# Six gathered rows in each ring instead of four, and the group loops written out, in a transformer encoder layer with expert retrieval

## The chip, the cores and the metric

The program runs on one core of a Trainium2 chip. Its time is the device time of one execution in microseconds (us); below it is the median of three executions. Beside them stands one profiled execution, from which all rows come.

## The reference, cut to what matters

The layer takes 1024 tokens of width 1024 in float32. It normalises them, projects them, runs 8-head latent attention and a 2-D Fourier transform side by side, mixes the two by sigmoid gates, projects, and normalises again (h1). Then comes the retrieval, from which nearly all memory traffic stems:

```python
q = (xt @ w_q).reshape(T, 8, 2, 128)
s_half = jnp.einsum('thcd,hcnd->thcn', q, keys)      # 128 keys per half
sv, si = lax.top_k(s_half, 16)
cand = (sv[:, :, 0, :, None] + sv[:, :, 1, None, :]).reshape(T, 8, 256)
cv, ci = lax.top_k(cand, 16)
expert = (ia * 128 + ib).reshape(T, 8 * 16)          # 128 experts of 16384 per token
gate = jax.nn.softmax(cv, axis=-1).reshape(T, 128)
u = jnp.take(w_u, ec, axis=0)                        # rows of 1024 floats
h = jnp.einsum('cd,ced->ce', xc, u)
a = jax.nn.gelu(h, approximate=False) * gc
y = jnp.einsum('ce,ced->cd', a, jnp.take(w_v, ec, axis=0))
out = layer_norm(alpha * h1 + y)
```

Each of the 1024 tokens needs 128 rows of `w_u` and 128 rows of `w_v`, of 4 KB each: 1.07 GB in all.

## The kernel before, in words

**Tiling.** 128 tokens are a tile, two tiles a group (`TILES`), and there are four groups (`GROUPS`). A prologue computes what all groups need (normalised input, latents, keys K and values V, the Fourier stage). Everything before the retrieval of a group is its *front*; the retrieval sums are its *peer* part. The peer part of group g runs beside the front of group g+1.

**Steps.** A group has 256 steps (`STEPS`), one for each of 2 x 128 slots; a slot is one expert for each of the 128 tokens of a tile. In each step m every engine does, in an order written out in its own program, first its piece of the peer part and then its piece of the front. Engines meet only in semaphores, and each runs its list strictly in order.

The peer piece of a step:
- GpSimd (POOL) issues a gather of 128 rows of `w_u` (`gather_u`, L301) for slot m + 76 and one of `w_v` (`gather_v`, L311) for slot m + 64 (`LEAD` 64, `AHEAD` 12). A gather is an indirect DMA of 512 KB, one 4 KB row to each partition.
- VectorE (DVE) multiplies the u row with h1 and sums it to one number per token (`dot`, L865), and frees the row (`u_free`).
- ScalarE (ACT) applies gelu to 8 slots at a time (L1083), and scales the v row by the coefficient into `av` (`scale`, L1092), which frees the v row (`scaled`).
- TensorE (PE) adds `av` to the accumulator by eight 128x128 transposing matmuls (L592).

**The rings.** Gathered rows lie in two rings, `u_rows` of `NU` = 4 and `v_rows` of `NV` = 4 rows, which share the tensor `rows`. A gather into a ring waits until the row four slots back has been used. On POOL the u gather and the v gather of a step follow one another in one queue, so that a u gather that waits for its row holds up the v gather behind it.

**The front by steps.** Steps 0 to 63 hold attention: a unit of one head and one tile every 4 steps, with scores (PE L475), row maximum (DVE L752), exponential (ACT L1023), transposes (PE L333), a copy (DVE L760) and the product with V (PE L491). For the first tile's eight units a query projection goes before (PE L459, taken out by ACT L1018 and DVE L744). Steps 72 to 119 hold gates and mixing (PE L515, L527, DVE L775), steps 120 to 135 the output projection (L538), from 136 the second normalisation, from 148 the retrieval's query and key scores (PE L559, L567) and the top-16 searches on DVE (`retrieve`, L726 to L854). The second tile's search of a group runs in the steps of the next group.
Weights come in a stream of 52 chunks per group on the SP queue through a ring of four (L244 waits, the next line loads). At step 0 of each group ACT loads the group's queries and rotary table (`load_queries`, L946 and L947), for which PE's first query projection waits.

**Loops.** POOL, PE, DVE and ACT run groups 0 to 2 of the peer part in a hardware loop (`Fori`), with semaphore counts computed in registers, and the last group written out; SP loops over all four groups. The steps before the first group's peer part (`peer(-1, ...)`, front of group 0) are written out as well. Before each gather there is a `nop` which carries the wait.

Of the kernel before, what the change touches and what calls it, by code (L numbers as in the profile page):

```python
# [25 lines left out]
FG, FD = 4, 128  # L26
PH, NK, HALF, TOPK = 8, 128, 128, 16
P = 128
# [11 lines left out]
LEAD = 64  # L40
PAIRS = PH // 2
PSLOTS = SLOTS // PAIRS
NU = NV = 4
NAV = 2
NW = 4
NDFT = 4
# [21 lines left out]
def layer_program(nc, x, lnp, w_lat, w_z, w_kr, b_lat, b_zT, b_krT, gqkv, w_uk, w_uv, b_gate, wstream,  # L68
# [4 lines left out]
    with ctx:  # L73
        def sb(name, shape, dt=fp32):
            return ctx.enter_context(nc.sbuf_tensor(name, shape, dt))
# [34 lines left out]
        bg = sb("bg", [P, 2, KD])  # L110
        rowsum = sb("rowsum", [P, TILES, H])
        rrow = sb("rrow", [P, TILES, H])
        nmax = sb("nmax", [P, 2])
        sv = sb("sv", [P, TILES, 2 * PH, TOPK])
        si = sb("si", [P, TILES, 2 * PH, TOPK], u32)
        cv = sb("cv", [P, TILES, PH, TOPK])
# [1 line left out]
        cab = sb("cab", [P, 2, PSLOTS])  # L118
        cabi = sb("cabi", [P, 2, PSLOTS], u32)
        iota16 = sb("iota16", [P, TOPK])  # L120
        altern = sb("altern", [P, 1])
        ymid = sb("ymid", [P, FG])
        gsum = sb("gsum", [P, 2])
        ids_peer = sb("ids_peer", [P, TILES, SLOTS], i32)
        gate_front = sb("gate_front", [P, TILES, SLOTS])
        gate_peer = sb("gate_peer", [P, TILES, SLOTS])
# [1 line left out]
        act_out = sb("act_out", [P, 2, BATCH])  # L128
        coef = sb("coef", [P, 2, BATCH])
        st = sb("st", [P, 3, 12])  # L130
        mv = sb("mv", [P, 3, 2])
        sd = sb("sd", [P, 3, 2])
        rq = sb("rq", [P, 4])
        gqk = sb("gqk", [P, 2, 2])
        bz = sb("bz", [P, FG])
        bkr = sb("bkr", [P, 1])

        s2_flat = S2[:, :, :, :].rearrange("p t c n -> p t (c n)")
        probs, probsT = s2_flat[:, 0, 0:S], s2_flat[:, 0, S:2 * S]
# [2 lines left out]
        onehot = sb("onehot", [P, PSLOTS, TOPK])  # L142


        hT_all = rows
        zcs = rows[:, :, :].rearrange("p t (g c) -> p t g c", g=FG)
        zT = hh
        w_lat_sb = S2[:, :, :, :].rearrange("p t c n -> p (t c n)").rearrange("p (k n) -> p k n", k=KD)
        w_z_sb = wring[:, :, :].rearrange("p a b -> p (a b)").rearrange("p (k n) -> p k n", k=KD)
# [74 lines left out]
        def positive(v):  # L224

            return not isinstance(v, int) or v > 0

        def slot_of(g, i):

            return (g + 1, i - STEPS) if i >= STEPS else (g, i)  # L230
# [10 lines left out]
        @block.sync  # L241
        def _(sp):
            def load(dst, src, s):
                sp.dma_start(dst, src).then_inc(s, 16)  # L244

            load(ident[:, :], ident_in, consts_in)
            load(x_t[:, 0, :], x[tok(0), :], x_in[0])
            for j in range(3):
                load(ln0[:, j, :], lnp[j:j + 1, :].to_broadcast([P, D]), ln0_in)
            load(blat, b_lat[0:1, :].to_broadcast([P, 512]), ln0_in)  # L250
            load(w_lat_sb, w_lat, w_lat_in)
            load(x_t[:, 1, :], x[tok(1), :], x_in[1])
            for dst, src in ((gqk[:, :, :], gqkv), (bz[:, :], b_zT), (bkr[64:128, :], b_krT),
                             (bg[:, :, :], b_gate), (iota16[:, :], iota_in), (dftc, dft_ch), (altern[:, :], altern_in)):
                load(dst, src, consts_in)
            load(w_z_sb, w_z, w_z_in)
            load(w_kr_sb, w_kr, w_z_in)
            load(w_uk_sb, w_uk, w_kv_in)
            load(w_uv_sb, w_uv, w_kv_in)
            load(rope_all[64:128, :], rope_tab, rope_in)  # L260
            for i in range(2, TT):
                sp.wait_ge(h0_done, i - 1)
                load(x_t[:, i % 2, :], x[tok(i), :], x_in[i % 2])
            sp.wait_ge(h0_done, TT)
            load(keys_sb, peer_keys.rearrange("c n d -> n c d"), keys_in)


            def stream(g):
                for c in range(CHUNKS):
                    sp.wait_ge(w_free, g * CHUNKS + c + 1)  # L270
                    n = 512 if c < WM0 else D
                    load(wring[:, c % NW, 0:n], wstream[c, :, 0:n], w_in_s[c % NW])

            sp.wait_ge(z_ps, 2 * FG)
            with sp.Fori(0, GROUPS) as g:
                stream(g)


# [1 line left out]
        def _(pool):  # L280
# [13 lines left out]
            def gather_u(g, i):  # L294
                g, i = slot_of(g, i)
                if i % PSLOTS == 0:
                    pool.wait_ge(handed, g * TILES * PAIRS + i // PSLOTS + 1)
                pool.wait_ge(u_free, g * STEPS + i + 1)
                pool.nop(nofuse=True)
                t, s = divmod(i, SLOTS)  # L300
                pool.indirect_dma_start(  # L301
                    u_rows[:, i % NU, :], None, peer_u,
                    bass.IndirectOffsetOnAxis(ap=ids_peer[:, t, s:s + 1], axis=0)).then_inc(u_in[i % NU], 16)

            def gather_v(g, i):
                g, i = slot_of(g, i)

                pool.wait_ge(scaled, g * STEPS + i + 1)
                pool.nop(nofuse=True)
                t, s = divmod(i, SLOTS)  # L310
                pool.indirect_dma_start(  # L311
                    v_rows[:, i % NV, :], None, peer_v,
                    bass.IndirectOffsetOnAxis(ap=ids_peer[:, t, s:s + 1], axis=0)).then_inc(v_in[i % NV], 16)

            def peer(g, last):
                for m in range(STEPS):
# [3 lines left out]
                        gather_v(g, m + LEAD)  # L320

            peer(-1, False)
            with pool.Fori(0, GROUPS - 1) as g:
                peer(g, False)
            peer(GROUPS - 1, True)

# [2 lines left out]
        def _(pe):  # L329
# [273 lines left out]
            for m in range(STEPS):  # L603
# [1 line left out]
                    peer(-1, m + LEAD)  # L605
                front(0, m)
                dft(m)
            with pe.Fori(0, GROUPS - 1) as g:
                for m in range(STEPS):
                    for t in range(TILES):  # L610
                        if m + LEAD == (t + 1) * SLOTS:
                            turn_back(g, t)
                    peer(g, m + LEAD)
                    front(g + 1, m)
# [8 lines left out]
        def _(dve):  # L623
# [169 lines left out]
            def retrieve(g, t, m, t0, period):  # L793

                for h in range(PH):
                    a = t0 + period * h
                    for c in range(2):
                        if m == a + c:
                            if c == 0:
                                dve.wait_ge(s_sb, g * 2 * PH + 2 * h + 2)  # L800
                                dve.nop(nofuse=True)
                            topk(S2[:, t, 2 * h + c, :], sv[:, t, 2 * h + c, :], si[:, t, 2 * h + c, :])
                    if m == a + 2:
                        dve.drain()
# [54 lines left out]
            def dot(g, i):  # L859
                g, i = slot_of(g, i)  # L860
                t = i // SLOTS
                dve.wait_ge(u_in[i % NU], g * (16 * STEPS // NU) + 16 * (i // NU + 1))
                row = u_rows[:, i % NU, :]
                b = i // BATCH % 2
                v.tensor_tensor_reduce(out=row, in0=row, in1=h1_peer[:, t, :], scale=1.0, scalar=0.0, op0=ALU.mult,  # L865
                                       op1=ALU.add, accum_out=dots[:, b, i % BATCH:i % BATCH + 1]).then_inc(u_free, 1)
# [61 lines left out]
                    if not last:  # L928
                        front(g + 1, m)

            with dve.Fori(0, GROUPS - 1) as g:
                group(g, False)
            group(GROUPS - 1, True)

# [2 lines left out]
        def _(act):  # L937
# [147 lines left out]
            def scale(g, i):  # L1085
                g, i = slot_of(g, i)
                if i % BATCH == 0:
                    act.wait_ge(coef_done, g * (STEPS // BATCH) + i // BATCH + 1)
                act.wait_ge(v_in[i % NV], g * (16 * STEPS // NV) + 16 * (i // NV + 1))
                act.wait_ge(av_free, g * STEPS + i + 1)  # L1090
                b = i // BATCH % 2
                s.activation(av[:, i % NAV, :], v_rows[:, i % NV, :], ACT.Copy,  # L1092
                             scale=coef[:, b, i % BATCH:i % BATCH + 1]).then_inc(scaled, 1)

            def evict(g, t):
# [53 lines left out]
                        if m + LEAD == (t + 1) * SLOTS + 2:  # L1149
                            store(g, t)  # L1150

            with act.Fori(0, GROUPS - 1) as g:
                group(g, False)
            group(GROUPS - 1, True)
            act.wait_ge(stored, 16 * (TT + 1))
# [84 lines left out]
```

## Time and profile before

| what | value |
|---|---|
| median of 3 executions | 3776.41 us (3761.76, 3776.41, 3784.91) |
| the profiled execution's own time | 3791.07 us |
| its span, first to last instruction | 3789.0 us |
| mean granted TensorE clock | 0.808 of full speed |
| busy, share of the span | PE 74%, PE weight loads 58%, DVE 59%, ACT 43%, POOL 62% |
| moved by DMA | 1241.31 MB, 328 GB/s over the span |
| of it by the gathers (queue 0) | 1073.87 MB |

The busy shares are means over stages with different limits. The gathers run from 541.9 us to the end, so that the share of POOL within that stretch is larger than 62%. A row of a wait says which engine and line waited for which; a row of the chain is a piece of the work that ended last.

### The profile page before, as it was taken

To read this page: it belongs to the slowest core of one execution; us is meant where nothing else is said; L and a number is where in the kernel's file an instruction comes from. 1 tells how busy PE (TensorE), PEld (TensorE's weight loads), DVE (VectorE), ACT (ScalarE), POOL (GpSimd) and SP (SyncE) were. 2 spreads that over 40 slices of the span, in tenths; PEclk is the share of its full clock that TensorE was granted. 3 is DMA by queue.
4 is the path that set the end of the run, shared out by engine and by line. 5 is a ranking of instruction groups with operands and counts; after the bars stand their busy time and mean duration, and the time that the engine had idled before them with its cause. 6 is when DMAs were issued, how large, how long until landed. Compare 5 with 4: busy or idle time off the path is not lost.

```text
span 3789.0 us, 45875 instructions
## 1 busy us (share of the span) xinstructions
PE 2797.3 (74%) x14008; PEld 2205.7 (58%) x14008; DVE 2224.2 (59%) x5004; ACT 1619.1 (43%) x1842; POOL 2342.6 (62%) x2075
## 2 busy tenths in 40 slices
PE   6999976677788676577788776677787776665666
PEld 3455855556676565466675665466675665554554
DVE  5143057457765686367666685467765685466643
ACT  1121014445454454355454454455454454444444
POOL 4000017766567778666667777666667777777775
PEclk9999987578799897588799896688898985555556
DMA  4224449989999999989999999899999999999998
GB/s 166 87 100 162 154 149 340 359 317 319 326 404 408 395 382 356 355 313 321 345 400 407 387 388 355 326 325 318 368 398 408 387 376 364 379 362 340 355 390 313
DMA packets 350484, 1241.31 MB, mean 328 GB/s; under 512 B 38481, under 2 KB 46161, under 8 KB 349713
## 3 DMA queue, kind: packets, MB, share of 16 engines
q0 software_dynamic: 294912, 1073.87, 75.6%
q1 hardware_dynamic: 34096, 117.94, 8.5%
q10 hardware_dynamic: 21216, 46.40, 3.4%
q8 instruction: 119, 1.95, 0.2%
q14 instruction: 141, 1.15, 0.1%
HBM read 1222.33 MB, written 15.73 MB: 327 GB/s over the span
## 4 chain that ended last, share of the span: by engine, by line
issue 25%; DMA 25%; PE 20%; POOL 11%; DVE 9%; ACT 5%; DVEq 4%; POOLq 0%; SPq 0%; ACTq 0%
DMA rows<-in_peer_v,ids_peer 15%; DMA rows<-in_peer_u,ids_peer 8%; POOL rows L311 5%; POOL rows L301 5%; ACT av L1092 3%; PE acc L592 3%; DVE rows L865 3%; PE fA L515 2%; PE fA L475 2%; PE m L363 2%; PE fB L527 1%; PE acc L581 1%; PE m L559 1%; DVE nmax L752 1%; PE fB L333 1%
## 5 line engine op out<-in xcount | busy, mean ns | idle before, releaser
L592 PE MATMUL acc<-ident,av 128*128 128x128 f32 x8192 | 1476.5, 340 | 873.9 <-ACT av L1092 860.2
L592 PEld LDWEIGHTS acc<-ident,av 128*128 128x128 f32 x8192 | 1208.8, 176 | 1162.1 <-ACT av L1092 1097.0
L1092 ACT ACTIVATE av<-rows,coef 128x1024 f32<-128x1024 f32 x1024 | 1168.2, 1146 | 1330.4 <-DMA rows<-in_peer_v,ids_peer 1235.1
L865 DVE CUSTOM_DVE_ANT_0 rows<-rows,hh 128x1024 f32<-128x1024 f32 x1024 | 1244.1, 1223 | 786.1 <-DMA rows<-in_peer_u,ids_peer 769.4
L301 POOL DMA_INDIRECT rows<-in_peer_u,ids_peer x1024 | 1110.4, 1084 | 926.5 <-DVE ids_peer L845 348.9
L311 POOL DMA_INDIRECT rows<-in_peer_v,ids_peer x1024 | 1184.2, 1156 | 356.5 <-issue 305.5
L559 PE MATMUL m<-hT_g,wring 128*128 128x256 f32 x1024 | 251.5, 402 | 1.1 <-ACT hT_g L1054 1.1
L515 PE MATMUL fA<-hT_g,wring 128*128 128x256 f32 x1024 | 236.2, 386 | 0.0
L559 PEld LDWEIGHTS m<-hT_g,wring 128*128 128x128 f32 x1024 | 204.5, 205 | 30.4 <-ACT hT_g L1054 1.5
L515 PEld LDWEIGHTS fA<-hT_g,wring 128*128 128x128 f32 x1024 | 195.2, 195 | 25.7
L1023 ACT ACTIVATE S<-fA,nmax 128x1024 f32<-128x1024 f32 x64 | 71.3, 1114 | 191.2 <-DVE nmax L754 191.1
L491 PEld LDWEIGHTS m<-V,S 128*128 128x128 f32 x1024 | 127.3, 201 | 11.4 <-issue 7.2
L760 DVE COPY S<-fB 128x1024 f32<-128x1024 f32 x64 | 78.2, 1221 | 94.5 <-PE fB L333 92.5
L491 PE MATMUL m<-V,S 128*128 128x64 f32 x1024 | 128.3, 281 | 3.4 <-DVE S L760 3.4
L475 PE MATMUL fA<-KT,hT_g 96*128 96x512 f32 x256 | 127.3, 621 | 0.0
L527 PE MATMUL fB<-yo,wring 128*128 128x256 f32 x512 | 121.4, 392 | 0.0
L752 DVE TENSOR_REDUCE nmax<-fA 128x1 f32<-128x1024 f32 x64 | 78.3, 1224 | 67.9 <-PE fA L475 67.9
L527 PEld LDWEIGHTS fB<-yo,wring 128*128 128x128 f32 x512 | 99.6, 198 | 13.7
L1083 ACT ACT_TABLE_LOAD x76 | 97.5, 1283 | 1.3
L775 DVE TENSOR_TENSOR prod<-sg,fB 128x512 f32<-128x512 f32 x32 | 21.9, 685 | 128.2 <-PE fB L527 128.0
L1062 ACT ACTIVATE qcT<-m 128x256 f32<-128x256 f32 x64 | 24.5, 383 | 148.4 <-PE m L559 148.4
L333 PE MATMUL fB<-ident,S 128*128 128x128 f32 x512 | 83.4, 318 | 1.0 <-issue 0.8
(153 smaller groups left out, 2190.8 us busy)
## 6 DMA issues: line engine op xcount, KB each, us to landing
wring<-in_wstream SPq DMA_DIRECT2D x192, 512.0 KB, 6.8
ln<-in_dft_seq ACTq DMA_DIRECT2D x32, 512.0 KB, 3.6
rows<-in_peer_u,ids_peer POOLq DMA_INDIRECT x1024, 6.5
rows<-in_peer_v,ids_peer POOLq DMA_INDIRECT x1024, 6.6
hT_g<-in_x SPq DMA_DIRECT2D x8, 512.0 KB, 4.0
hres_spill<-KT ACTq DMA_DIRECT2D x8, 512.0 KB, 2.7
hT_spill<-rows ACTq DMA_DIRECT2D x1, 4096.0 KB, 11.1
wring<-in_wstream SPq DMA_DIRECT2D x16, 256.0 KB, 6.0
```

The costliest lines, as they stand in the source:

```text
L301: pool.indirect_dma_start(u_rows[:, i % NU, :], None, peer_u, bass.IndirectOffsetOnAxis(ap=ids_peer[:, t, s:s + 1], axis=0)).then_inc(u_in ...
L311: pool.indirect_dma_start(v_rows[:, i % NV, :], None, peer_v, bass.IndirectOffsetOnAxis(ap=ids_peer[:, t, s:s + 1], axis=0)).then_inc(v_in ...
L333: return nc.tensor.transpose(out_, in_, ident[:, :])
L475: last = mm(fA[:, half * 512:(half + 1) * 512], qT_g[0:QK, h, tok(qt)], KT[0:QK, h, half * 512:(half + 1) * 512], start=True, stop=True)
L491: last = mm(m1[:, h * VD:(h + 1) * VD], probsT[:, tok(k)], V[:, k, h * VD:(h + 1) * VD], start=k == 0, stop=k == TT - 1)
L515: last = mm(gb[:, j * GROUP:(j + 1) * GROUP], w[:, tok(k)], hT_g[:, k, :], start=k == 0, stop=k == KD - 1)
L527: last = mm(yb[:, j * GROUP:(j + 1) * GROUP], w[:, tok(4 * j + k)], src[:, k, :], start=k == 0, stop=k == 3)
L559: last = mm(m0[:, (qc % 2) * GROUP:(qc % 2 + 1) * GROUP], w[:, tok(k)], hT_g[:, k, :], start=k == 0, stop=k == KD - 1)
L592: last = mm(acc[:, tok(k)], av[:, i % NAV, tok(k)], ident[:, :], is_transpose=True, start=i % SLOTS == 0 and k % 4 == 0, stop=i % SLOTS == ...
L752: v.reduce_max(nmax[:, u % 2:u % 2 + 1], fA[:, :], AX)
L865: v.tensor_tensor_reduce(out=row, in0=row, in1=h1_peer[:, t, :], scale=1.0, scalar=0.0, op0=ALU.mult, op1=ALU.add, accum_out=dots[:, b, i ...
L1092: s.activation(av[:, i % NAV, :], v_rows[:, i % NV, :], ACT.Copy, scale=coef[:, b, i % BATCH:i % BATCH + 1]).then_inc(scaled, 1)
```

## The change

`NU` and `NV` go from 4 to 6. The tensor `rows` has one pool of `NU + NV` rows and so grows from 8 to 12 rows, 16 KB more per partition. The space comes from two places: the DMA scratch of the program is set to 4096 bytes per partition (its default is 16384), and ten small tensors, each of which was padded on its own, become slices of one. `hT_all` and `zcs`, which used all of `rows`, use its first 8 rows.

256 steps are no multiple of 6, so that the ring's row and its semaphore count depend on the group: `ring` and `landed` work them out from the slot's number over all groups. With loops that would need registers, so the loops are written out as Python loops in all five programs, with constants for all counts. The `nop` ahead of each gather, and one on DVE before a top-16 search, go.

```diff
-NU = NV = 4
+NU = NV = 6
...
+        small = sb("small", [P, 34])
+        nmax = small[:, 0:2]
...
-        hT_all = rows
-        zcs = rows[:, :, :].rearrange("p t (g c) -> p t g c", g=FG)
+        hT_all = rows[:, 0:KD, :]
+        zcs = hT_all.rearrange("p t (g c) -> p t g c", g=FG)
...
+        def ring(g, i, n):
+            return (g * STEPS + i) % n
+        def landed(g, i, n):
+            return 16 * ((g * STEPS + i) // n + 1)
...
-            with sp.Fori(0, GROUPS) as g:
+            for g in range(GROUPS):
                 stream(g)
...
                 pool.wait_ge(u_free, g * STEPS + i + 1)
-                pool.nop(nofuse=True)
                 t, s = divmod(i, SLOTS)
                 pool.indirect_dma_start(
-                    u_rows[:, i % NU, :], None, peer_u,
-                    bass.IndirectOffsetOnAxis(ap=ids_peer[:, t, s:s + 1], axis=0)).then_inc(u_in[i % NU], 16)
+                    u_rows[:, ring(g, i, NU), :], None, peer_u,
+                    bass.IndirectOffsetOnAxis(ap=ids_peer[:, t, s:s + 1], axis=0)).then_inc(u_in[ring(g, i, NU)], 16)
...
                 pool.wait_ge(scaled, g * STEPS + i + 1)
-                pool.nop(nofuse=True)
...
-            with pool.Fori(0, GROUPS - 1) as g:
+            for g in range(GROUPS - 1):
                 peer(g, False)
...
-            with pe.Fori(0, GROUPS - 1) as g:
+            for g in range(GROUPS - 1):
...
                                 dve.wait_ge(s_sb, g * 2 * PH + 2 * h + 2)
-                                dve.nop(nofuse=True)
...
-                dve.wait_ge(u_in[i % NU], g * (16 * STEPS // NU) + 16 * (i // NU + 1))
-                row = u_rows[:, i % NU, :]
+                dve.wait_ge(u_in[ring(g, i, NU)], landed(g, i, NU))
+                row = u_rows[:, ring(g, i, NU), :]
...
-                act.wait_ge(v_in[i % NV], g * (16 * STEPS // NV) + 16 * (i // NV + 1))
+                act.wait_ge(v_in[ring(g, i, NV)], landed(g, i, NV))
                 act.wait_ge(av_free, g * STEPS + i + 1)
...
-    nc = bacc.Bacc("TRN2", target_bir_lowering=False, num_devices=1)
+    nc = bacc.Bacc("TRN2", target_bir_lowering=False, num_devices=1, dynamic_dma_scratch_size=4096)
```

## Rows read from the trace of the kernel before

**Rows 1.** The page: GB/s moved in each of 40 equal slices of the span.
```profile
GB/s 166 87 100 162 154 149 340 359 317 319 326 404 408 395 382 356 355 313 321 345 400 407 387 388 355 326 325 318 368 398 408 387 376 364 379 362 340 355 390 313
```

**Rows 2.** Groups of instructions: count | busy us, mean ns | idle before, its releasers. The gathers.
```profile
L311 POOL DMA_INDIRECT rows<-in_peer_v,ids_peer x1024 | 1184.2, 1156 | 356.5 <-issue 305.5 <-ACT av L1092 38.8 <-DVE dots L865 12.2
L301 POOL DMA_INDIRECT rows<-in_peer_u,ids_peer x1024 | 1110.4, 1084 | 926.5 <-DVE ids_peer L845 348.9 <-DVE dots L865 280.8 <-issue 252.2
```

**Rows 3.** Stretches: length, busy us of PE, PEld, DVE, ACT, POOL, clock, DMA share, GB/s.
```profile
542.00:800.00 258.00, 162.41 (x751) 132.37 (x750) 155.99 (x384) 99.34 (x113) 178.86 (x158) 0.66 0.92 335
800.00:1050.00 250.00, 188.52 (x1104) 157.79 (x1103) 179.82 (x389) 129.51 (x144) 157.69 (x146) 0.84 0.92 327
1050.00:1250.00 200.00, 163.82 (x904) 130.02 (x901) 121.69 (x268) 97.80 (x102) 140.29 (x125) 0.99 1.02 406
1250.00:1600.00 350.00, 239.80 (x1280) 202.57 (x1280) 220.83 (x532) 164.76 (x186) 264.98 (x232) 0.77 0.98 372
1600.00:1850.00 250.00, 184.15 (x1043) 152.49 (x1044) 173.19 (x360) 127.53 (x144) 151.85 (x139) 0.80 0.89 315
1850.00:2050.00 200.00, 168.78 (x926) 139.15 (x925) 121.29 (x289) 99.14 (x104) 144.48 (x125) 0.97 1.01 398
2050.00:2400.00 350.00, 245.59 (x1307) 204.34 (x1306) 229.01 (x545) 167.93 (x189) 267.62 (x236) 0.79 0.99 381
2400.00:2700.00 300.00, 213.32 (x1209) 175.50 (x1210) 198.06 (x421) 148.40 (x165) 183.07 (x170) 0.81 0.89 318
2700.00:2900.00 200.00, 167.04 (x905) 133.70 (x903) 119.62 (x267) 97.23 (x101) 141.92 (x124) 0.97 1.02 401
2900.00:3400.00 500.00, 344.99 (x1727) 286.37 (x1727) 315.14 (x745) 232.70 (x252) 386.79 (x344) 0.70 0.99 376
3400.00:3789.00 389.00, 244.44 (x1108) 196.70 (x1106) 208.57 (x456) 170.32 (x167) 276.93 (x255) 0.60 0.94 351
```

**Rows 4.** Timeline of POOL: start, duration, instruction [idle before]; first in a loop, then written out.
```profile
2398.32 1.01 POOL L301 DMA_INDIRECT rows<-in_peer_u,ids_peer  x1 [0.30 <-issue]
...
3501.48 0.93 POOL L301 DMA_INDIRECT rows<-in_peer_u,ids_peer  x1 [0.30 <-issue]
```

**Rows 5.** Who waited for whom: us in total, times, longest; the two gather waits, 2400 to 2700.
```profile
ACT av L1092 <- DMA rows<-in_peer_v,ids_peer: 70.8, 38, 5.4
POOL rows L301 <- DVE dots L865: 67.9, 27, 8.6
```

**Rows 6.** Timeline of PE in the attention steps of the third loop pass.
```profile
2451.30 1.88 PE L475 MATMUL fA<-KT,hT_g 96*128 96x512 f32 x4
...
2457.01 1.85 PE L592 MATMUL acc<-ident,av 128*128 128x128 f32 x8 [1.21 <-ACT av L1092]
2458.65 1.91 PE L459 MATMUL m<-cqT_g,wring 128*128 128x256 f32 x4
2462.07 1.10 PE L592 MATMUL acc<-ident,av 128*128 128x128 f32 x8 [1.50 <-ACT av L1092]
...
2464.75 1.88 PE L475 MATMUL fA<-KT,hT_g 96*128 96x512 f32 x4
```

**Rows 7.** The chain that ended last, in order of time, shortly after: start, us, what.
```profile
2474.10 9.01 DMA rows<-in_peer_v,ids_peer
...
2492.39 1.73 PE fA L475 x4
```

**Rows 8.** The chain at the loop's turn, around 2412 us.
```profile
2412.41 2.58 issue
...
2421.56 8.03 DMA rope_g<-in_rope_tab
```

**Rows 9.** From issue to landing of the u gathers, all of them.
```profile
DMA to landing us min/median/max: 4.1/6.5/12.0
```

**Rows 10.** The page: the queues that fetch the program's instructions: packets, MB, share.
```profile
q8 instruction: 119, 1.95, 0.2%
q14 instruction: 141, 1.15, 0.1%
```

More of the change, by code:

```diff
@@ L112, in layer_program @@
         rrow = sb("rrow", [P, TILES, H])
-        nmax = sb("nmax", [P, 2])
         sv = sb("sv", [P, TILES, 2 * PH, TOPK])
@@ L120, in layer_program @@
         iota16 = sb("iota16", [P, TOPK])
-        altern = sb("altern", [P, 1])
-        ymid = sb("ymid", [P, FG])
-        gsum = sb("gsum", [P, 2])
         ids_peer = sb("ids_peer", [P, TILES, SLOTS], i32)
@@ L130, in layer_program @@
         st = sb("st", [P, 3, 12])
[L131 to L136, printed above, removed]
+        small = sb("small", [P, 34])
+        nmax = small[:, 0:2]
+        altern = small[:, 2:3]
+        ymid = small[:, 3:7]
+        gsum = small[:, 7:9]
+        mv = small[:, 9:15].rearrange("p (a b) -> p a b", b=2)
+        sd = small[:, 15:21].rearrange("p (a b) -> p a b", b=2)
+        rq = small[:, 21:25]
+        gqk = small[:, 25:29].rearrange("p (a b) -> p a b", b=2)
+        bz = small[:, 29:33]
+        bkr = small[:, 33:34]
         s2_flat = S2[:, :, :, :].rearrange("p t c n -> p t (c n)")
@@ L308, in gather_v @@
                 pool.wait_ge(scaled, g * STEPS + i + 1)
-                pool.nop(nofuse=True)
                 t, s = divmod(i, SLOTS)
                 pool.indirect_dma_start(
-                    v_rows[:, i % NV, :], None, peer_v,
-                    bass.IndirectOffsetOnAxis(ap=ids_peer[:, t, s:s + 1], axis=0)).then_inc(v_in[i % NV], 16)
+                    v_rows[:, ring(g, i, NV), :], None, peer_v,
+                    bass.IndirectOffsetOnAxis(ap=ids_peer[:, t, s:s + 1], axis=0)).then_inc(v_in[ring(g, i, NV)], 16)
             def peer(g, last):
@@ L929, in group @@
                         front(g + 1, m)
-            with dve.Fori(0, GROUPS - 1) as g:
+            for g in range(GROUPS - 1):
                 group(g, False)
@@ L1088, in scale @@
                     act.wait_ge(coef_done, g * (STEPS // BATCH) + i // BATCH + 1)
-                act.wait_ge(v_in[i % NV], g * (16 * STEPS // NV) + 16 * (i // NV + 1))
+                act.wait_ge(v_in[ring(g, i, NV)], landed(g, i, NV))
                 act.wait_ge(av_free, g * STEPS + i + 1)
                 b = i // BATCH % 2
-                s.activation(av[:, i % NAV, :], v_rows[:, i % NV, :], ACT.Copy,
+                s.activation(av[:, i % NAV, :], v_rows[:, ring(g, i, NV), :], ACT.Copy,
                              scale=coef[:, b, i % BATCH:i % BATCH + 1]).then_inc(scaled, 1)
@@ L1150, in group @@
                             store(g, t)
-            with act.Fori(0, GROUPS - 1) as g:
+            for g in range(GROUPS - 1):
                 group(g, False)
```

## The prediction

> **What bounds the kernel now.** I read the slices of the page first. Up to slice 6 the rate is 87 to 166 GB/s, from then on 313 to 408 [rows 1]: the kernel is a prologue of 542 us and then 3247 us of gathering. The change touches the prologue only in where tensors lie, so the question is what sets the pace behind it.
>
> The second view is the two gather groups on POOL [rows 2]. A gather costs POOL 1.084 us (u) or 1.156 us (v), and before each of them there is a gap of 0.30 us in which nothing is waited for [rows 4]. So 2048 gathers take 1110 + 1184 + 2048 x 0.30 = 2909 us of POOL's queue, out of 3247 us. POOL is within 10% of being the bound by itself, which its 62% of the span hides.
>
> The third view splits the 3247 us by stage [rows 3]. For each stretch I take length - POOL busy - 0.30 x its gathers: that is what POOL really stood idle.
> - Attention (800 to 1050, 1600 to 1850, 2400 to 2700): 48.5, 56.5 and 65.9 us idle, 171 us together, at only 315 to 327 GB/s.
> - Gates and projection (1050 to 1250, 1850 to 2050, 2700 to 2900): 22, 18 and 21 us idle, 61 us together, at 398 to 406 GB/s. No slice of the page goes above 408: here the transfers are the bound, and POOL waits because rows come late.
> - The search steps (1250 to 1600, 2050 to 2400, 2900 to 3400): 15, 12 and 10 us idle, 37 us together. POOL is the bound, at 372 to 381 GB/s.
> - The start (542 to 800): 32 us. The end (3400 to 3789): 36 us, of which about 20 lie behind the last gather.
>
> So more rows in flight can help only where POOL waits for a row, and only if neither the transfers nor another chain of work sets the pace there.
>
> **The attention stretches** hold half of the idle time, and look like a shortage of rows: from 2400 to 2700 POOL waited 67.9 us for dots, and ACT 70.8 us for v rows [rows 5]. But whose wait is on the path? A unit is 4 steps. From one score matmul (2451.30) to the next (2464.75) are 13.45 us. In it PE waits 1.21 and 1.50 us for ACT's scaling [rows 6], and what ACT was behind both times is the front itself: scores, maximum on DVE, exponential, then the scaling that is next on ACT's list; and the query projection, which ACT takes out before it scales. No gather is in that circle. The next units do have one, a v gather of 9.01 us [rows 7], and yet the scores of 2451.30 and 2492.39 [rows 6, 7] lie 41.1 us apart for three units, 13.7 us each. The gather wait runs beside a chain that is almost as long. A unit loses about 0.3 us by it on that evidence.
>
> **The change, part by part.**
> - *Rings in attention.* 16 units a group at 0.3 us would be 5 us; the second tile's units also wait for DVE's searches and vary more, so I take 0.5 us each: 8 us a group, 24 us for three groups. The ends are 0 and all of POOL's idle time, 171 us. I stay near the low end, as the unit without a gather is the row that fits the pace.
> - *Leaving attention.* POOL is held up by full rings there, so with six it enters the next stage two slots further on in each ring. Those four gathers (2.1 MB) were moved while there was room, and need not be moved in the stage at the ceiling: 2.1 MB at 408 GB/s is 5.1 us a group, 15 us for three. Bounds 0 and twice that.
> - *Gates and projection.* Transfers bind. From a mean of 402 to 408 GB/s would be 1.5% of 600 us, 9 us; I take 6.
> - *Search steps.* The 37 us are short waits at tile ends and in DVE's searches. A ring two slots deeper absorbs waits shorter than two steps, which are four gathers of POOL at 1.42 us, 5.7 us; transfers have 7% room to 408 GB/s. I take 20, bounds 0 and 37.
> - *Start and end.* Of 32 and 16 us, 11: the first gathers are limited by four rows, but also by the front beside them.
> - *Loops written out.* At the turn of the loop POOL's chain shows 2.58 us of issue [rows 8]. Two turns, an entry and an exit: 8 us, bounds 0 and 15. Inside the pass registers and counts cost nothing visible: the gap before a gather is 0.30 us in the loop and in the written-out group alike [rows 4]. For the same reason I cost the removed `nop` at nothing: the gap stays the same with register arithmetic ahead of it or none. If it did save the 0.03 us of one queue entry, 2048 times, that would be 61 us; that end goes into the range. The code fetch stays as it is: 3.10 MB were fetched for 45,875 instructions [rows 10], 68 bytes each, so passes through a loop are already fetched each time. If fetching did stall, it would be in the written-out last group, where POOL runs without a pause.
> - *A moved load.* The rotary load at step 0 takes 8.03 us on the path [rows 8], among at most 8 gathers in flight. With up to 12 it may take 2 us longer: -6 us for three groups, bounds 0 and -12.
> - *Weight stream on SP.* It too lands later, but three chunks are loaded ahead, at least six steps of about 3 us; the cover is larger than the 12 us of the slowest gather's landing [rows 9]. Nothing.
> - *Packed small tensors, a moved `rows`.* No engine's work changes. Nothing.
> - *Scratch.* Up to 8 gathers are in flight with 16384 bytes, and no row shows POOL waiting for room; with a quarter of it and 12 in flight no row of this trace can say. Nothing, with a rival below.
>
> Gain: 24 + 15 + 6 + 20 + 11 + 8 - 6 = 78 us. The profiled execution took 3791.07 us, 14.7 us above the median of 3776.41. Against its own time the changed kernel comes to 3713, against the median to 3698.
>
> On the scratch, the Trainium skill (DMA: Bandwidth & Descriptors, The descriptor swizzle) says that a 128-partition transfer writes 9 read and 9 write descriptors on each engine, of 16 bytes each; by that my estimate is 256 places, 28 gathers, in the smaller scratch, and it would not bind. No run here shows it yet.
>
> **Rivals.**
> - *The rings are the bound in attention* (20%). For it: 171 us of idle POOL, and the chain through a 9 us v gather. Against it: the 13.45 us unit. If it holds, attention gives back its 171 us instead of 24: 225 us in all, 3551 by the median. The floor of this case: each stretch of [rows 3] takes the longer of its length less POOL's idle time and its bytes at 408 GB/s. From the first stretch to the last that is 226, 202, 199, 335, 194, 195, 338, 234, 197, 490 and 373 us, 2982 in place of 3247, 265 us saved: 3511. With 130 us saved it is 3646.
> - *Nothing moves* (21%). Transfers and POOL bind wherever the front does not, the stored slots are given back in the next stage, and only the loop turns are saved: 3738 to 3790. It would also come so if the transfers were at their ceiling over the whole stretch. The 11 stretches move 1171 MB in 3247 us, 361 GB/s; were that the ceiling, no ring could help: 3776. Against it stand 398 to 406 GB/s for 200 us on end, three times [rows 3]; it has 3 of the 21%. The Trainium skill (SBUF — State Buffer, Summary: rules for kernel authors) says to estimate HBM to SBUF by about 358 GB/s; by that the 1171 MB would need 3271 us and the kernel would already stand at the bound. The trace, with 406 GB/s, disagrees.
> - *The smaller scratch holds POOL up* (9%), the case on the other side. Place: each gather, on POOL. It decides when the scratch has room for fewer gathers than the rings. If room is what 8 in flight just fitted in, a quarter holds 2, and a gather could be issued every 4.1 / 2 = 2.05 us at the shortest landing [rows 9]: 542 + 2048 x 2.05 = 4740 us. With room for 4 at the median landing it is 6.5 / 4 = 1.63 us each, 3870 us by the profiled execution, 3855 by the median. It would show as idle time of POOL with no row free to blame, and longer gathers.
>
> **How the numbers follow.** The forecast's own case (gain 40 to 120 us) has 50% and gives 3656 to 3736; the rings as bound 20%; nothing 21%; slower 9%. A change of 1% (38 us) is about what a measurement of this kernel can tell from none. Faster by more than that is the first two cases, 70%; within 1%, 21%; slower, 9%. The range of 3600 to 3785 leaves out the deep end of the second case, half of its chance, and the slower one. The 61 us of the `nop` would move the forecast to 3637, within it.
>
> **What would show it.** Right: attention stretches still at about 13.2 to 13.6 us a unit, with ACT's wait for v rows mostly gone and POOL still idle there; the search steps without POOL idle time; gates at 405 GB/s or above with the gathers' landing longer than the 6.5 us of before; the 2.6 us of issue at the turns gone. Wrong: units of 12 us or less in attention (the ring was the bound), a gap before gathers other than 0.30 us (the `nop` or the scratch), or gathers longer than 0.94 us without DVE beside them.

## The result, and the profile after

The changed kernel took 3664.82 us (median of 4 runs, 3655.13 to 3692.76) against 3769.09 us before on the same chip (3759.08 to 3784.91): ratio 0.9735, 95% interval 0.970 to 0.977. By the ratio that is 100 us; the two medians lie 104 us apart. The forecast was 3698 us, within 3600 to 3785; the gain was 78 us forecast and 100 us measured. The profiled execution took 3666.81 us, its span is 3665.0 us, 124 us shorter than the profiled span of before. The profiled execution of before was the slowest of its four and 22 us above their median, so what is read from these two traces adds up to more than the 100 us.

First the page, the slices of the changed kernel, as in [rows 1]:

```profile
GB/s 170 92 92 144 172 125 341 384 344 327 330 399 409 409 409 386 376 340 317 360 409 409 409 393 376 374 338 328 373 409 409 409 382 373 408 364 357 359 396 344
```

Ten slices now stand at 408 or 409 GB/s where two of before reached 408, and none goes above. The troughs of 317 to 344 GB/s are still there. They are the attention steps.

The two gather groups, as in [rows 2] (count | busy us, mean ns | idle before):

```profile
L310 POOL DMA_INDIRECT rows<-in_peer_u,ids_peer x1024 | 1151.3, 1124 | 828.2 <-DVE ids_peer L852 348.9 <-issue 276.0 <-DVE dots L872 203.3
L319 POOL DMA_INDIRECT rows<-in_peer_v,ids_peer x1024 | 1156.7, 1130 | 318.9 <-issue 278.1 <-ACT av L1099 40.8
```

POOL's wait for dots fell from 281 to 203 us, and that number still holds the 0.30 us of each gap. To have POOL's time exactly, I took all 2048 gathers of the timeline and split the time from the first to the last into their lengths, gaps of 0.30 us, and what is left:

| kernel | gathers' lengths | gaps | POOL idle | profiled run |
|---|---|---|---|---|
| before | 2296 us | 617 us | 312 us | 3791.07 us |
| after | 2309 us | 617 us | 176 us | 3666.81 us |

The gain is POOL's idle time, 136 us, less 13 us by which the gathers became longer in sum. The gap is the same 617 us without the `nop`, with constants and in a quarter of the scratch:

```profile
2301.93 0.94 POOL L319 DMA_INDIRECT rows<-in_peer_v,ids_peer  x1 [0.30 <-issue]
2303.18 1.01 POOL L310 DMA_INDIRECT rows<-in_peer_u,ids_peer  x1 [0.30 <-issue]
```

Where in the steps did the time come from? PE's rows give marks that are the same steps in both kernels: the first and last scores of a group, the first output projection, the first query projection of the retrieval, and its last one. A mark is the start of such a block of matmuls. The sums are worked out from the timelines.

| stretch (sum over groups) | before | after | gain |
|---|---|---|---|
| first gather to first scores of group 1 | 246.3 | 234.3 | 12 |
| scores, first to last (3 groups) | 614.9 | 595.8 | 19 |
| last scores to output projection (3) | 591.1 | 568.9 | 22 |
| output projection (3) | 255.5 | 253.3 | 2 |
| retrieval queries, first to last (3) | 546.1 | 524.8 | 21 |
| last query to the next group's first scores, over the turn (2) | 310.7 | 290.1 | 21 |
| last query of group 3 to the end | 682.6 | 657.5 | 25 |

With the 2 us by which the first gather came sooner that is the 124 us between the two spans.

Two attention stretches of the changed kernel and one of gates, columns as in [rows 3]:

```profile
1570.00:1767.00 197.00, 154.92 (x920) 130.29 (x918) 140.77 (x287) 108.98 (x125) 132.98 (x120) 0.84 0.93 328
2361.00:2559.00 198.00, 155.58 (x917) 131.47 (x916) 140.72 (x287) 108.67 (x124) 133.85 (x119) 0.83 0.92 327
2559.00:2749.00 190.00, 155.41 (x907) 136.24 (x906) 135.83 (x332) 98.45 (x107) 141.97 (x118) 0.94 1.00 390
```

And the waits in the third group's attention (who waited for whom: us in total, times, longest). The first four lines are the kernel before, from 2437 to 2643, the first to the last scores; the others are the changed kernel, from 2361 to 2559:

```profile
PE acc L592 <- ACT av L1092: 51.4, 35, 3.3
POOL rows L301 <- DVE dots L865: 43.6, 20, 3.6
ACT av L1092 <- DMA rows<-in_peer_v,ids_peer: 41.8, 25, 4.1
ACT S L1023 <- DVE nmax L754: 32.0, 15, 3.7
```

```profile
ACT S L1030 <- DVE small L762: 53.7, 15, 6.5
PEld acc L600 <- ACT av L1099: 46.7, 26, 3.4
PE acc L600 <- ACT av L1099: 39.0, 26, 3.3
POOL rows L310 <- DVE dots L872: 34.5, 21, 3.4
```

The stretch of [rows 5] is 100 us longer, as it holds the turn and the first gates, and its 70.8 us are 41.8 us here. This wait of ACT for v rows has gone from the list altogether. But ACT now waits 22 us more for the row maximum from DVE (53.7 instead of 32.0 us), and POOL still waits for dots. So ACT's waits for rows were removed, and the attention steps became 3% shorter.

The gates can be split further. From the first gate matmul to the output projection 63.2, 63.4 and 63.3 MB were moved in 157.4, 158.8 and 161.3 us before, and 61.9, 62.1 and 61.5 MB in 153.3, 153.9 and 152.9 us after. Each group thus moves 1.5 MB less there, about three gathers, at 403 instead of 398 GB/s. At the ceiling the missing bytes are 11 us for three groups, and the better rate 6 us.

The turn of the loop, as in [rows 8], from the chain that ended last:

```profile
2337.13 1.01 POOL rows L310
2338.14 0.30 issue
2338.45 6.56 DMA rows<-in_peer_v,ids_peer
...
2345.68 8.22 DMA rope_g<-in_rope_tab
...
2353.94 2.09 PE m L467 x4
```

The 2.58 us of issue are gone. The rotary load takes 8.22 us instead of 8.03 and is still on the path; over the three groups it takes 8.40 instead of 8.27 us in the mean.

### The profile page after: what moved, and what is told of

Its sections match the earlier page's. It is cut to its first block, busy times and chain, and to the rows that moved or that the text cites. A ratio compares the mean times of both kernels' runs of the same rounds, so it can differ in the third digit from the quotient of the medians.

```text
span 3665.0 us, 40824 instructions
## 1 busy us (share of the span) xinstructions
PE 2779.8 (76%) x14008; PEld 2205.7 (60%) x14008; DVE 2220.9 (61%) x5004; ACT 1612.2 (44%) x1842; POOL 2356.0 (64%) x2075
## 3 DMA queue, kind: packets, MB, share of 16 engines
q0 software_dynamic: 294912, 1073.87, 76.7%
## 4 chain that ended last, share of the span: by engine, by line
POOL 29%; PE 24%; DMA 18%; issue 11%; DVE 8%; ACT 5%; DVEq 3%; SPq 0%; ACTq 0%; POOLq 0%
DMA rows<-in_peer_v,ids_peer 17%; POOL rows L310 15%; POOL rows L319 15%; PE acc L600 5%; ACT av L1099 4%; PE fA L483 3%; PE m L567 2%; PE fA L523 2%; PE m L371 2%; DVE small L760 2%; PE acc L589 1%; PE fB L341 1%; DVE rows L872 1%; PE m L467 1%; PE m L499 1%
## 5 line engine op out<-in xcount | busy, mean ns | idle before, releaser
L310 POOL DMA_INDIRECT rows<-in_peer_u,ids_peer x1024 | 1151.3, 1124 | 828.2 <-DVE ids_peer L852 348.9
L319 POOL DMA_INDIRECT rows<-in_peer_v,ids_peer x1024 | 1156.7, 1130 | 318.9 <-issue 278.1
L1030 ACT ACTIVATE S<-fA,small 128x1024 f32<-128x1024 f32 x64 | 71.3, 1114 | 266.1 <-DVE small L762 266.1
L768 DVE COPY S<-fB 128x1024 f32<-128x1024 f32 x64 | 78.2, 1222 | 100.2 <-PE fB L341 98.6
L760 DVE TENSOR_REDUCE small<-fA 128x1 f32<-128x1024 f32 x64 | 78.3, 1223 | 53.0 <-PE fA L483 52.9
L783 DVE TENSOR_TENSOR prod<-sg,fB 128x512 f32<-128x512 f32 x32 | 21.8, 682 | 121.5 <-PE fB L535 121.5
```

The source lines that it names most:

```text
L310: pool.indirect_dma_start(u_rows[:, ring(g, i, NU), :], None, peer_u, bass.IndirectOffsetOnAxis(ap=ids_peer[:, t, s:s + 1], axis=0)).then_ ...
L319: pool.indirect_dma_start(v_rows[:, ring(g, i, NV), :], None, peer_v, bass.IndirectOffsetOnAxis(ap=ids_peer[:, t, s:s + 1], axis=0)).then_ ...
L760: v.reduce_max(nmax[:, u % 2:u % 2 + 1], fA[:, :], AX)
```

## The experiments

Each kernel is the changed one with one edit, unless it says otherwise. The runs fell in three sessions, each on another chip. In the first the kernel before took 3944.41 us, in the second 3774.78 us, in the third 3771.07 us; so times are compared within a session, and ratios are to the kernel before of the same session. Why the first chip takes 4.5% longer for the same program is not known. The first session has r4, r5, u6v4 and u4v6, the second b4, r4b, r6 and u6v4b, the third the rest.

**1. Everything but the rings.**

```diff
-NU = NV = 6
+NU = NV = 4
```

> The changed kernel with four rows in each ring (everything else of the change kept: loops written out, no nop, small scratch, packed tensors). Theory (the rings gave nearly all): 0 to 12 us below the kernel before (ratio 0.997 to 1.000), about 95 us above the changed kernel; POOL idle about 300 us between gathers. Rival (written-out loops and the missing nop gave it): 60 us or more below the kernel before, ratio 0.985 or less, gap before gathers below 0.30 us.

> Four rows in each ring, loops written out, again, now beside the whole change. Theory: 8 to 40 us below the kernel before; its distance to the six-row kernel is what the rings give.

Measured: 3893.36 against 3944.41 us, ratio 0.9906 (0.9867 to 0.9944), and in the second session 3754.11 against 3774.78 us, ratio 0.9945 (0.9925 to 0.9965). So what is not the ring is worth 51 us in the first session, between theory and rival, and 21 us (13 to 28 by the interval) in the second, more than the 8 us that I had allowed. Of the three sessions the whole change ran in the second only. There it lies another 80 us below: that is the rings, four fifths of the gain.

**2. The kernel before and the whole change in the same session,** for their traces.

> The kernel before, unchanged, for a trace from the same chip as the three beside it. Theory: POOL idle between gathers is larger than in the four-row kernel with written-out loops only around the loop's turns (3 to 4 us at each of two turns, an entry and an exit). Rival (registers cost time inside the passes): the surplus is spread over all stages of groups 1 to 3.

> The whole change. Theory after the first four runs (the u ring gives nearly all, the v ring nothing): same time as six u rows with four v rows within 10 us, 55 to 75 us below the four-row kernel. Rival (both rings are needed for the full gain): 20 us or more below six-and-four.

Measured: 3773.17 us (one run) and 3673.69 us, ratio 0.9737 (0.970 to 0.9775): the gain stood again. POOL's account for the second session, made as above:

| kernel | lengths | gaps | idle | profiled run |
|---|---|---|---|---|
| before | 2286 us | 617 us | 305 us | 3773.17 us |
| rings of 4 | 2271 us | 617 us | 278 us | 3732.11 us |
| u 6, v 4 | 2324 us | 616 us | 193 us | 3698.95 us |
| u 6, v 6 | 2315 us | 617 us | 174 us | 3671.15 us |

(The profiled run of the kernel with rings of 4 is the fastest of its 11; their median is 3754 us.) The table shows the rings' work and a part that is given back: idle time falls by 104 us from the second line to the fourth, but the gathers' lengths grow by 44 us. How large the part is stays open: from the kernel before to the whole change they grow by 29 us here and by 13 us in the first pair of traces.

The same marks as above, in us gained, split the gain into the rings and the rest (b4 is the kernel before, r4b the one with rings of 4, r6 the whole change):

| stretch | whole change (b4 to r6) | without the rings (b4 to r4b) | rings alone (r4b to r6) |
|---|---|---|---|
| first gather to first scores of group 1 | 11 | 3 | 8 |
| scores, first to last (3) | 6 | -10 | 17 |
| last scores to output projection (3) | 27 | 11 | 16 |
| output projection (3) | 3 | 2 | 1 |
| retrieval queries, first to last (3) | 24 | 12 | 12 |
| last query to the next scores, over the turn (2) | 15 | 16 | -1 |
| last query of group 3 to the end | 15 | 8 | 8 |

What is not the ring gives most over the turn: 302.2 us for two groups in the kernel before against 285.9 us with the loops written out, 8 us a turn. In the prediction two turns, an entry and an exit were 8 us together. But the kernel with six u and four v rows, written out as well, takes 301.4 us over the two turns. Over the end, where both programs were written out already, b4 and r4b differ by 8 us too, which the loops can't explain. So a turn's cost of 8 us is not shown; single profiled executions differ by that much.

The whole change and six u rows with four v rows lie 27 us apart. My theory of within 10 us fell, and the rival held: both rings are needed for the full gain.

**3. Five rows.**

```diff
-NU = NV = 6
+NU = NV = 5
```

> Five rows in each ring. Theory (each further slot takes away the shorter part of POOL's waits): more than half of the ring's gain, 55 to 70 us below the kernel before, ratio 0.981 to 0.986. Rival (the ring acts as a threshold, latency over slots): 20 us or less, or already all of it.

Measured: 3854.73 us, ratio 0.9804 (0.9718 to 0.9889), 39 us below the kernel with rings of 4 of its session. It lies 90 us below the kernel before, where I had expected 55 to 70, and the rival's threshold is not to be seen. The 39 us are half of the 80 us that two slots gave in the other session, which would make each slot worth as much; but six rows in both rings did not run beside them in the first session, so that is likely and not shown.

**4. One ring alone.**

```diff
-NU = NV = 6
+NU, NV = 6, 4
```

> Six u rows, four v rows. Theory (POOL is one queue: it runs ahead only as far as the shorter ring allows): under a third of the gain, 0 to 35 us below the kernel before, with POOL's waits moved from the u gather (for dots) to the v gather (for ACT's scaling). Rival (POOL waited for dots 281 us and for scaling 83 us, so the u ring is what counts): 70 us or more of gain.

> Six u rows, four v rows, again, beside the whole change. Theory (u ring alone): within 10 us of the whole change; POOL's wait moves to ACT's scaling but shrinks in sum. Rival: 20 us or more above it.

```diff
-NU = NV = 6
+NU, NV = 4, 6
```

> Four u rows, six v rows. Theory (shorter ring decides): 0 to 35 us below the kernel before, POOL's wait for dots stays near 280 us. Rival (ACT's wait for v rows was on the path, 1235 us in all): 60 us or more of gain.

Measured: six u rows alone 3827.48 us, ratio 0.974 (0.9659 to 0.9821), 66 us below rings of 4; in the second session 3701.14 us, ratio 0.9799 (0.9752 to 0.9846), 53 us below. Six v rows alone 3933.32 us, ratio 0.9972 (0.9924 to 1.0021), 40 us above rings of 4. My theory, that the shorter ring decides, fell with the first of the two kernels: the u ring alone gives two thirds of the rings' 80 us, and the v ring gives the other 27 us when the u ring is long. The second kernel came as expected, with a wait for dots of 361 us. Why it is even slower than rings of 4, by 40 us, the record does not show. The waits in the kernel with six u and four v rows, over the whole kernel:

```profile
POOL rows L319 <- ACT av L1099: 244.2, 247, 8.5
POOL rows L319 <- issue: 237.2, 777, 0.6
...
POOL rows L310 <- DVE dots L872: 28.2, 19, 3.3
```

and in the one with rings of 4:

```profile
POOL rows L310 <- DVE dots L872: 315.8, 180, 11.0
...
POOL rows L319 <- ACT av L1099: 53.0, 123, 1.9
```

The wait did move to the v gather, as I said, but it shrank on the way: from 369 to 272 us, both gathers together. POOL comes to a free v row sooner than to a free u row. That this is because DVE is the later of the two engines in most steps fits the two lists, but no run tested it.

**5. Do transfers or landing times set the pace?** Gathers of 1 KB instead of 4 KB per row; the other three quarters of each row are zeros, set once. The row numbers stay as they are, so all pieces come from the first quarter of each table.

```diff
+        peer_u_q = peer_u.rearrange("e (a d) -> (e a) d", a=4)
...
-                    u_rows[:, ring(g, i, NU), :], None, peer_u,
+                    u_rows[:, ring(g, i, NU), 0:256], None, peer_u_q,
```

and the same for v.

> The changed kernel with gathers of 128 x 1 KB instead of 4 KB; the other three quarters of each row are left out (zeros, set once, some 10 us on POOL), all else stays. Theory (the transfers bind only in the gates and projection stretches; elsewhere POOL and the front): 20 to 60 us below the changed kernel, POOL without a pause in nearly all stretches but attention, attention units still 13 us. Rival (landing time of 7 us is the limit in most stretches): 150 us or more below.

Measured: 3585.9 us (two runs), ratio 0.9511 (0.9475 to 0.9548), about 85 us below the changed kernel: above the 60 us of the theory and far from the rival. The stretches from its profile, attention, gates and retrieval queries of group 3:

```profile
2350.00:2548.00 198.00, 153.65 (x897) 133.23 (x897) 153.67 (x343) 105.47 (x119) 137.21 (x117) 0.80 0.34 102
2590.00:2730.00 140.00, 126.86 (x699) 100.33 (x698) 93.79 (x208) 76.61 (x80) 110.76 (x97) 0.99 0.59 181
2810.00:2990.00 180.00, 131.72 (x710) 111.72 (x709) 135.83 (x355) 90.33 (x106) 143.45 (x121) 0.80 0.38 111
```

By the marks attention takes 197.6, 198.1 and 198.3 us, with a third of the transfers' rate. The changed kernel takes 200.8, 196.7 and 198.3. So in the attention of the changed kernel the transfers are not on the path, nor is the wait for rows: the front is. The gates, first gate matmul to output projection, take 138.7, 138.4 and 138.2 us instead of 153.3, 153.9 and 152.9: there the transfers bind, and cost 15 us a group. The retrieval queries take 176.8, 176.5 and 178.2 us, no less than in the changed kernel (176.3, 174.6, 173.9), and POOL is without idle time: there POOL binds.

**6. What makes a gather on POOL longer?** Half of POOL's gathers take 0.94 us, a quarter more than 1.2. In the changed kernel's timelines (start, us, engine line op [idle before]) of POOL and DVE, around one of the long ones:

```profile
2313.41 1.02 POOL L310 DMA_INDIRECT rows<-in_peer_u,ids_peer  x1 [0.30 <-issue]
2314.73 0.94 POOL L319 DMA_INDIRECT rows<-in_peer_v,ids_peer  x1 [0.30 <-issue]
2315.97 1.77 POOL L310 DMA_INDIRECT rows<-in_peer_u,ids_peer  x1 [0.31 <-issue]
```

```profile
2312.39 1.23 DVE L872 CUSTOM_DVE_ANT_0 rows<-rows,hh 128x1024 f32<-128x1024 f32 x1 [1.33 <-DMA rows<-in_peer_u,ids_peer]
...
2315.70 1.23 DVE L872 CUSTOM_DVE_ANT_0 rows<-rows,hh 128x1024 f32<-128x1024 f32 x1 [2.08 <-DMA rows<-in_peer_u,ids_peer]
```

The first gather and the third begin while a dot runs, and end 0.81 us after the dot does (2313.62 to 2314.43, 2316.93 to 2317.74). The second meets no dot and takes 0.94 us. In the same trace 496 of the 517 gathers above 1.2 us begin while a dot runs, and 16 more beside a comparison on DVE that reads two SBUF operands (L840, 0.69 us). The test: the dot reads one SBUF operand instead of two, in the same time; the product with h1 is left out, and nothing is written back over the row.

```diff
-                v.tensor_tensor_reduce(out=row, in0=row, in1=h1_peer[:, t, :], scale=1.0, scalar=0.0, op0=ALU.mult,
-                                       op1=ALU.add, accum_out=dots[:, b, i % BATCH:i % BATCH + 1]).then_inc(u_free, 1)
+                v.reduce_sum(dots[:, b, i % BATCH:i % BATCH + 1], row, AX).then_inc(u_free, 1)
```

> The changed kernel with the dot on DVE (two SBUF inputs, 1.23 us) replaced by a plain sum of the row (one SBUF input, 1.22 us in the same place); the product with h1 is left out. Theory (a gather issued while a dot runs waits for the dot's end): gathers shorten from 1.13 to about 0.95 us, POOL's queue needs 2048 x 1.25 = 2560 us, and the kernel lies 100 to 180 us below the changed kernel, at 3490 to 3570 us on a chip with the kernel before at 3770, then held by transfers at 409 GB/s and by attention. Rival (the longer gathers are POOL's own, or the transfers already bind): lengths stay, within 30 us of the changed kernel.

Measured: 3587.18 us (two runs), ratio 0.9515 (0.9477 to 0.9553), about 84 us below the changed kernel, short of the 100 to 180 us. The mechanism held. From its trace, first a gather beside the comparison that still reads two operands, then one beside the sum that took the dot's place:

```profile
893.47 1.33 POOL L310 DMA_INDIRECT rows<-in_peer_u,ids_peer  x1 [1.14 <-DVE dots L872]
...
3302.24 0.95 POOL L310 DMA_INDIRECT rows<-in_peer_u,ids_peer  x1 [0.30 <-issue]
```

```profile
893.29 0.69 DVE L840 TENSOR_TENSOR onehot<-cab,iota 128x512 f32<-128x512 f32 x1
...
3301.81 1.22 DVE L872 TENSOR_REDUCE dots<-rows 128x1 f32<-128x1024 f32 x1 [1.34 <-DMA rows<-in_peer_u,ids_peer]
```

The comparison ends at 893.98, and its gather 0.82 us later; the sum ends at 3303.03, and its gather 0.16 us later, which is 0.95 us after its own start. The edit takes away the write of the row along with the second operand, but the write is not the cause: in the changed kernel's trace the 26 gathers that begin beside the copy of L768, which writes 1024 numbers a partition from PSUM, take 0.94 us, and so do the 18 beside the product of L783, whose second input lies in PSUM.

```profile
L310 POOL DMA_INDIRECT rows<-in_peer_u,ids_peer x1024 | 984.0, 961 | 1048.2 <-DVE dots L872 510.1 <-DVE ids_peer L852 348.2 <-issue 189.9
L319 POOL DMA_INDIRECT rows<-in_peer_v,ids_peer x1024 | 965.2, 943 | 372.4 <-issue 234.4 <-ACT av L1098 136.5 <-DVE dots L872 1.5
```

The lengths in sum fell from 2309 to 1952 us, 357 us of POOL's queue; but POOL's idle time rose to 450 us, and only a quarter of what was freed came through. The page says what took over, with 17 slices at 408 or 409 GB/s:

```profile
GB/s 170 98 82 160 159 112 356 409 354 351 335 407 409 409 409 407 409 314 319 353 409 409 409 409 407 381 343 329 360 409 409 409 408 405 409 408 373 409 409 339
...
rows<-in_peer_u,ids_peer POOLq DMA_INDIRECT x1024, 11.9
```

The u gathers now take 11.9 us to land instead of 7.1: they queue at the transfers' ceiling. Behind POOL's bound lies that of the transfers, and in attention that of the front, about 85 us further on.

The Trainium skill (SBUF — State Buffer, Who interferes with whom) says that a DVE instruction with two SBUF inputs contends with a GpSimd instruction that reads SBUF, and that one with a single SBUF input does not, outside certain modes. By that rule this case's traces agree: 1.77 us beside the two-input dot, 0.95 us beside the one-input sum. The same section reports that such a two-input instruction did not stall DMA in an earlier probe; for these gathers, which read their row numbers from SBUF, the measured 1.77 us decides.

**7. The load that stays on the path.** The next group's queries and rotary table are loaded at step 63 of the group before.

```diff
-                if m == 0 and positive(g):
-                    act.wait_ge(handed, (g * TILES - 1) * PAIRS)
-                    load_queries(g)
...
                     act.wait_ge(scores_ps, (g + 1) * TILES * H)
+                    if g + 1 < GROUPS:
+                        load_queries(g + 1)
```

> The changed kernel with the next group's queries and rotary table loaded at step 63 of the group before instead of at step 0. Theory (three times PE waits 6 to 7 us for this load at the turn, ahead of the front-bound attention): 15 to 24 us below the changed kernel, ratio to the kernel before 0.967 to 0.970. Rival (the six-row rings or POOL's backlog absorb the wait): within 6 us of the changed kernel, 0.972 to 0.975.

Measured: 3657.94 us, ratio 0.9712 (0.9685 to 0.9739), 13 us less than the 3671 us that the changed kernel's ratio of 0.9735 would be in the third session. PE's waits for this load, 18.7 us in the changed kernel's trace of the second session, are gone from the list, and POOL's idle time is 142 us instead of 174. The ratio lies between theory and rival. The intervals of the two ratios overlap, and the two ran in different sessions, so that the gain is likely but not shown. Its ratio is the lowest of all versions with the reference's full work.

**8. The scratch alone,** on the kernel before.

```diff
-    nc = bacc.Bacc("TRN2", target_bir_lowering=False, num_devices=1)
+    nc = bacc.Bacc("TRN2", target_bir_lowering=False, num_devices=1, dynamic_dma_scratch_size=4096)
```

> The kernel before with only the DMA scratch cut from 16384 to 4096 bytes. Theory (a quarter of the scratch still has room for all gathers in flight): no change, ratio 0.997 to 1.003. Rival (POOL waits for room): slower by 1% or more, with gaps above 0.30 us or longer gathers.

Measured: 3760.2 us against 3771.07, ratio 0.9977 (0.9957 to 0.9996). The smaller scratch costs nothing with at most 8 gathers in flight; that it costs nothing with 12 rests on the changed kernel's gaps, which are 617 us in all, as ever. The interval just misses 1 on the fast side. Perhaps 9 of the 21 us of experiment 1 lie here, where `rows` and all else move to other addresses; no run tells what of it is real.

## Why the prediction was right, point by point

- *Rings in attention*: 24 us forecast, 19 measured in the first pair of traces; the rings alone gave 17 in the second session, the whole change 6. The reasoning from the 13.45 us unit held: units took 13.66 us before and 13.24 after in the mean of 45, and experiment 5 showed the same length of stretch with a quarter of the bytes. The rival that the rings bound here, with 171 us to be had, fell; it would have been the natural reading of 67.9 us of POOL waiting.
- *Leaving attention and the gates*: 15 + 6 us forecast, 22 measured. The split holds too: about 11 us are bytes that were moved earlier, 6 us the better rate, and 4 us lie between attention and the gates. The ceiling was read rightly from the slices: no slice of any kernel's page goes above 410 GB/s.
- *Search steps*: 20 forecast; 21 from first to last query and 2 in the output projection. Between the last query and the next scores lie 21 more, which the second session gives to what is not the ring. The rings alone gave 12 and 1 there.
- *Start and end*: 11 forecast, 12 at the start alone, and 25 at the end. This is one of two mis-sized terms. In the end stretch POOL's idle time fell by 11 us (16.1 to 5.3), and its 458 gathers became shorter, 1.102 to 1.070 us in the mean, another 15 us. I had taken their length as fixed. It is set by how often a gather meets a dot. In the second session the same stretch had 1.079 us before and 1.077 after, and gained 15 us. So of the 25 us some 10 are this execution's luck.
- *Loops written out*: 8 forecast, 21 measured for all that is not the ring, and 51 in the first session. I had seen the turn's 2.58 us on one engine; by the marks of b4 and r4b a turn costs 8 us, which other traces don't bear out (experiment 2). That several engines turn one after another and wait for each other would explain it, but was not tested. A part of up to 9 us may belong to the scratch. How the 21 us divide stays open.
- *The `nop`*: nothing forecast, and the gap stayed 0.30 us. No run took it away alone.
- *The rotary load*: 6 us lost forecast, next to none measured (8.27 to 8.40 us in the mean of three).
- *The scratch as a hold-up*: fell; experiments 2 and 8. By the estimate from the Trainium skill's page (DMA: Bandwidth & Descriptors, The descriptor swizzle), 28 gathers, the 12 in flight had room, and the traces agree: the gaps are the same, and the changed kernel's 294912 packets for 2048 gathers are 144 each, 9 on each of 16 engines.
- *The transfers at their ceiling all along*: fell with the gain, and with 409 GB/s in slices on end; the about 358 GB/s of the Trainium skill (SBUF — State Buffer, Summary: rules for kernel authors) are not what this kernel's traces show.
- A term was missing: what is given back. The rings took 104 us of POOL's idle time, but 44 us went into longer gathers by the traces of r4b and r6 (13 and 29 us by the two pairs with the kernel before).
- *The signs*: the attention units, ACT's wait for v rows, the turn's issue and the landing time (7.1 us over all, 14 us in the gates against 8 before) came as said. Two came in part: the gates moved 403 GB/s and not 405, and POOL kept some 8 of its 26 us idle time from first to last query.

The sum of 78 us against 100 us is thus right in its mechanism. In the second session the rings gave 80 us, where their terms with the rotary load's loss came to 70, and what is not the ring gave 21 us instead of 8. That single terms meet their stretches to a few us is in part luck, as two executions of one kernel differ by up to 12 us in a stretch (attention: 614.9 and 602.7 us in the two traces of the kernel before).

## What to carry to other kernels

Before a ring is made deeper, ask of each stretch who is late when the queue waits for a free row: where a whole unit of the consumer's own chain is as long as the pace, the ring gives little, however long the waits in the list (here 3% of the attention steps). A deeper ring takes short pauses away, and carries work from a stretch that has transfers to spare into one that has not. The list of stretches with idle time, the queue's own cost and the rate in each gave 78 of 100 us here. And count the length of an issue on its engine as something that other engines change.

## What the runs showed of the hardware

- A gather issued on GpSimd while a DVE operation runs that reads two SBUF operands ends 0.81 us after that operation does, or 0.94 us after its own start, whichever is later: 1.77 us in the example beside a dot of 1.23 us, up to 2.2 us. Of the 895 gathers of the changed kernel that begin beside a dot, 870 follow this within 0.02 us. Beside DVE operations with one SBUF input gathers take 0.94 us. Without the second operand the 2048 gathers took 357 us less of the queue, 11% of the stretch.
- Between two gathers lie 0.30 us, whatever stands between them: a wait with a `nop` and register arithmetic, a wait with a `nop`, or a wait alone.
- The transfers' ceiling is 409 to 410 GB/s for rows of 4 KB at random places: 17 slices of one page stand at 408 or 409, and none of any page above 410. The gathers landed in 6.5 us before, in 7.1 us with twelve in flight, and in 11.9 us once POOL no longer held them back.
- At a turn of the hardware loop POOL's chain shows 2.58 us of issue, and 0.30 us at the same place with the loops written out. What a turn costs the kernel is not shown.
